# Turning the norms: tokens on partitions, fp16 rows turned by DMA transposes, in a fused conv/gMLP/MLP block

## The reference, cut to what matters

```
h  = rmsnorm(x, norm1_g);  p = h @ w_in                  # 1024 -> 2560
y_a = b_gate * conv3(c_gate * xc)                        # 512 channels
y_b = u * spatial_gating(layernorm(v))                   # 512 channels
y  = concat(rmsnorm(y_a), rmsnorm(y_b))
x1 = x + y @ w_out                                       # 1024 -> 1024
h2 = rmsnorm(x1, norm2_g);  a = relu(h2 @ w_up)          # 1024 -> 4096
out = rmsnorm(x1 + (a * a) @ w_down, final_g)            # 4096 -> 1024
```

## Time and profile before

| | us |
|---|---|
| device time, 3 runs | 1275.43, 1275.84, 1279.14 |
| median | 1275.84 |
| span of the profiled execution, core 0, first to last instruction | 1233.4 |
| spans of the eight cores | 1226.8 to 1233.4 |
| what the median has beside that span | 42.4 |
| TensorE busy in the span | 1195.1 (97%) |
| VectorE busy | 939.3 (76%) |
| ScalarE busy | 533.5 (43%) |

### The profile page before, as it was taken

The page is one execution under the profiler, slowest core; times in us unless marked ns, Lnnn a source line. Parts: engine busy times, 40 slices in busy tenths (PEclk is TensorE's granted clock), DMA queues, the critical chain, the costliest instruction groups (busy, mean ns, idle before and its releaser), DMA issues.

```text
span 1233.4 us, 19511 instructions; the slowest of 8 cores (1226.8 to 1233.4 us)
## 1 busy us (share of the span) xinstructions
PE 1195.1 (97%) x6264; PEld 584.4 (47%) x6264; DVE 939.3 (76%) x1460; ACT 533.5 (43%) x905; POOL 82.0 (7%) x144
## 2 busy tenths in 40 slices
PE   5899999999999999999999999999999999999994
PEld 3345645546556464444444444444444444444442
DVE  2799889898899997448879747868746877856745
ACT  4554664555644555045047116217305417504533
POOL 0101011010001100001100100000000000100000
PEclk8999999999999999999999999999999999999998
DMA  7977888696676869357898954667964655975424
GB/s 184 163 162 197 202 219 202 175 258 153 176 234 182 294 219 301 119 183 174 222 309 270 282 204 159 212 199 223 296 230 150 218 185 172 296 252 179 150 90 137
DMA packets 60084, 253.87 MB, mean 206 GB/s; under 512 B 6224, under 2 KB 8400, under 8 KB 59984
## 3 DMA queue, kind: packets, MB, share of 16 engines
q1 hardware_dynamic: 38800, 182.36, 43.7%
q0 software_dynamic: 21184, 70.26, 25.9%
HBM read 211.71 MB, written 65.01 MB: 224 GB/s over the span
## 4 chain that ended last, share of the span: by engine, by line
PE 88%; DMA 8%; DVE 1%; issue 1%; ACT 1%; SPq 0%; DVEq 0%; ACTq 0%; POOLq 0%
PE PS L506 88%; DMA XS_92<-x_s 2%; DMA oT<-RA 1%; DMA RA<-x_s 1%; DMA WCXB_51<-wcxb 1%; DMA WV<-wv 1%; DMA X_75<-xT 1%; DMA WCXB_53<-wcxb 1%; DMA WSB_107<-wst 1%; DMA X_76<-xT 0%; DVE RB L522 0%; DVE RA L522 0%; SPq L533 0%; DVE H_93 L525 0%; ACT DUMP_57 L513 0%
## 5 line engine op out<-in xcount | busy, mean ns | idle before, releaser
L522 DVE TENSOR_TENSOR RB<-PS,RB 128x512 f32<-128x512 f32 x128 | 88.2, 690 | 84.6 <-PE PS L506 82.3
L522 DVE TENSOR_TENSOR RA<-PS,RA 128x512 f32<-128x512 f32 x96 | 66.0, 689 | 58.4 <-PE PS L506 55.6
L506 PE MATMUL PS<-YN,WO 128*128 128x256 f16 x896 | 104.7, 273 | 1.0 <-DVE YN L522 0.8
L522 DVE TENSOR_TENSOR A_86<-A_86 128x512 bf16<-128x512 bf16 (+1 forms) x192 | 93.9, 506 | 12.8 <-ACT A_86 L513 8.3
L506 PEld LDWEIGHTS PS<-YN,WO 128*128 128x128 f16 x896 | 87.3, 98 | 20.6 <-issue 2.8
L513 ACT ACTIVATE SN_88<-PS 128x512 f32<-128x512 f32 x63 | 37.2, 594 | 109.2 <-PE PS L506 108.7
L506 PE MATMUL PS<-A_86,RING_80 128*128 128x512 bf16 x308 | 76.7, 379 | 2.4 <-DVE RB L522 2.4
L506 PE MATMUL PS<-A_86,RING_82 128*128 128x512 bf16 x308 | 77.2, 379 | 0.0
L506 PE MATMUL PS<-A_86,RING_83 128*128 128x512 bf16 x308 | 77.1, 379 | 0.0
L506 PE MATMUL PS<-A_86,RING_81 128*128 128x512 bf16 x308 | 76.3, 379 | 0.0
L506 PE MATMUL PS<-H_93,RING_80 128*128 128x512 f16 x308 | 75.4, 379 | 0.0
(11 more groups left out here) (237 smaller groups left out, 2078.4 us busy)
## 6 DMA issues: line engine op xcount, KB each, us to landing
RING_80<-ws_s SPq DMA_DIRECT2D x20, 896.0 KB, 5.9
RING_81<-ws_s SPq DMA_DIRECT2D x20, 896.0 KB, 6.3
RING_83<-ws_s SPq DMA_DIRECT2D x20, 896.0 KB, 6.5
RING_82<-ws_s SPq DMA_DIRECT2D x20, 896.0 KB, 5.6
RING_84<-ws_s SPq DMA_DIRECT2D x20, 896.0 KB, 6.2
RING_85<-ws_s SPq DMA_DIRECT2D x20, 896.0 KB, 6.2
ws_s<-PREP_70 SPq DMA_DIRECT2D x12, 896.0 KB, 5.7
ws_s<-PREP_69 SPq DMA_DIRECT2D x12, 896.0 KB, 6.0
```

The source lines that it names most:

```text
L506: ins = e.matmul(real(o_), lhsT=l, rhs=r, start=st, stop=sp, skip_group_check=True)
L522: dve(lambda e: e.tensor_tensor(out=out, in0=real(in0), in1=in1, op=op), reads, writes, n, rate, in0)
```

## The change

x, x1 and the result are now kept with **tokens on partitions**: chunk `s` of a tile is 128 tokens x 1024 channels, `rows(b, s)`.

- Norms: a token's sum of squares is the accumulator of one ScalarE Square over its row, rstd a [128x1] or [128x4] column. `stats` with `ONESD` stays for tile 0 alone, which is still loaded transposed (`xT0`), and the `ONESE` sums of y stay.
- x of tiles 1 to 7: `normed_rows` casts to fp16 with rstd as the scalar, into one of two buffers `HTK`; `turn` is a DMA transpose on the SP queue from there into `HT`, 4 a tile of 256 KB. For tile m+2 this is done during tile m. Tile 0's x is loaded a second time, by rows, for the residual.
- x1: `out_proj` has YN stationary (128 tokens) and WO moving (512 columns), so 56 matmuls of 512 columns stand for 112 of 256. It squares, casts and stores h2 as fp16 rows (`h2_d`) beside x1; `h2_part` is two DMA transposes of 512 KB and eight in-place gain multiplies. `XS`, `RSL` and `rs_d` are gone.
- Down: A2 stationary, weights moving. The loop is product by product over 4 token chunks with 4 sets of banks; one ring load (1 MB) is one product's weights, 7 a phase in place of 8 of 896 KB. In the last phase the last four products go chunk by chunk, and each chunk is finished at once.
- 28 of the weight combinations are made in the mixer and 4 in the first up phase; `schedule` has 40 tries in place of 120; an operation `group` lets the four transposes into one HT buffer not wait for each other.

```diff
@@ new helpers
+        def turn(out, in_, reads, writes, dkey, nbytes, group=None, margin=1.0):
+            S.add("sp", lambda e: e.dma_start_transpose(out=out, in_=in_), reads=reads, writes=writes, dma_key=dkey,
+                  nbytes=nbytes, occ=0.6, margin=margin, packet=1.0, group=group)
+        def squares(b, s, dump, acc, key):
+            act(dump[:, :, :], b[:, 2 * s:2 * s + 2, :], AF.Square, b.keys(2 * s, 2), dump.keys(0, 2) + [key],
+                n=2 * MT + 170, accum_out=acc)
+        def x_norm(m):
+            b, h = X[(m + 1) % 3], HT[m % 2]
+            for s in range(4):
+                i, ap, keys = normed_rows(b, s, SSX[:, s:s + 1], [("ssx", s)], True)
+                turn(h[:, :, 128 * s:128 * s + 128], ap, keys, h.keys(0, 8), ("xt", i), 2 * 128 * 1024, group=("ht", m))
@@ out_proj
-            for dc in (0, 2):
+            for u in range(2):
...
+                    pe(bank, [(bank[:, :], YN[:, b, k, 128 * u:128 * u + 128], WO[:, a, k, :], first and k == 0,
+                               last and k == 3) for k in range(4)],
...
-            rs = RS1[nxt("rs", 3)] if m + 1 < NMT else RS7
-            rstd(rs[:, :], stats(x, X1Q, 8, ONESD), MT, rs.keys())
-            dma("sp", rs_d[m], rs[:, :], rs.keys(), [("rsd", m)], ("rss", m % 2), 4 * 128 * MT)
+                rstd_rows(SS1[:, 2 * u:2 * u + 2], 2, keys, keys)
+                for h in range(2):
+                    s = 2 * h + u
+                    i, ap, hk = normed_rows(x, s, SS1[:, 2 * u + h:2 * u + h + 1], [("ss1", u, h)])
+                    dma("sp", h2_d[m, 128 * s:128 * s + 128, :], ap, hk, [("h2d", m, s)], ("hs", i), 2 * 128 * 1024)
@@ h2_part
+            for kk in range(2):
+                q = ((3, 2), (4, 1))[kk][h]
+                turn(H2[:, q, :, :], h2_d[m, :, 512 * kk:512 * kk + 512], [("h2d", m, s) for s in range(4)], h2k(q),
+                     ("h2t", q), 2 * 512 * 512, margin=4.0)
+                for k in range(4):
+                    scale(H2[:, q, k, :], pcol(G2, 4 * kk + k), h2k(q, k), MT)
@@ down, in place of down_unit and final
+        def down(finish):
+            chains = [{P1: bA, P6: bA, P7: bA, P4: bA, P2: bD, P5: bC, P3: bC}
+                      for bA, bC, bD in (banks_acd() for _ in range(4))]
+            adds = {P1: (0, 0), P2: (0, 0), P5: (1, 1), P6: (1, 0), P3: (1, 0), P7: (1, 1), P4: (0, 1)}
+            def step(p, w, s):
+                a, b = p
+                bank = chains[s][p]
+                pe(bank, [(bank[:, :], A2[:, q, b, 128 * s:128 * s + 128], w[:, q, :], p in (P1, P2, P5) and q == 0,
+                           p in (P2, P3, P4) and q == 7) for q in range(8)],
+                   [x for q in range(8) for x in a2k(q, b)] + w.keys(0, 8))
+                h, d_ = adds[p]
+                b, j = R[h], 2 * s + d_
+                tt(b[:, j, :], bank[:, :], b[:, j, :], ALU.add, bank.keys() + b.keys(j), b.keys(j))
+            together = 7 if finish is None else 3
+            for p in ORDER[:together]:
+                w = RD[use(1)[0]]
+                for s in range(4):
+                    step(p, w, s)
+                refill(1)
+            if finish is not None:
+                ws = [RD[i] for i in use(4)]
+                for s in range(4):
+                    for p, w in zip(ORDER[3:], ws):
+                        step(p, w, s)
+                    finish(s)
+        def gains(g, s):
+            for h in (1, 0):
+                squares(R[h], s, DUMPF, SSF[:, 2 * s + h:2 * s + h + 1], ("ssf", s, h))
+                rstd_rows(SSF[:, 2 * s + h:2 * s + h + 1], 1, [("ssf", s, h)], [("ssf", s, h)])
+        def piece(g, s, after):
+            for h in (1, 0):
+                b = R[h]
+                for d_ in range(2):
+                    j = 2 * s + d_
+                    stt(b[:, j, :], b[:, j, :], SSF[:, 2 * s + h:2 * s + h + 1], GFR[:, d_, :], ALU.mult, ALU.mult,
+                        b.keys(j) + GFR.keys(d_) + [("ssf", s, h)] + after, b.keys(j))
+                dma("sp", oN[2 * g + h, s], rows(b, s), b.keys(2 * s, 2), [("out", 2 * g + h, s)], ("os", h, s),
+                    4 * 128 * 2 * MT)
@@ start
+        load_x(0, gate)
@@ tile loop
+            if m + 2 < NMT:
+                x_stats(m + 2)
...
+            if m + 2 < NMT:
+                x_norm(m + 2)
             out_proj(m)
```

More of the change, by code:

```diff
@@ L127, in add @@
         for k in reads:
-            w = self.last_w.get(k)
-            if w is not None:
+            for w in self.last_w.get(k, ()):
                 deps[id(w)] = w
         for k in writes:
-            w = self.last_w.get(k)
-            if w is not None:
+            joins = group is not None and self.groups.get(k, (None, None))[0] == group
+            for w in self.groups[k][1] if joins else list(self.last_w.get(k, ())) + self.readers.get(k, []):
                 deps[id(w)] = w
-            for r in self.readers.get(k, ()):
-                deps[id(r)] = r
         for k in reads:
@@ L139, in add @@
         for k in writes:
-            self.last_w[k] = op
+            if group is not None and self.groups.get(k, (None, None))[0] == group:
+                self.last_w[k].append(op)
+                continue
+            self.groups[k] = (group, list(self.last_w.get(k, ())) + self.readers.get(k, []))
+            self.last_w[k] = [op]
             self.readers[k] = []
@@ L549, in warm, with stats @@
             pe(bank, [(bank[:, 0:128], ONESD[:, :], ONESD[:, :], True, True)] * n, ONES + reads)
-        def stats(src, q, n, ones, rows=2, first=False, behind=[]):
+        def stats(src, q, n, ones, rows=2, first=False):
             bank = bank8()
@@ L582, in load_x, with load_first, rows @@
                     chain.append(landed)
-        def stage0_stats(m, behind=[]):
-            return stats(X[(m + 1) % 3], XQ[m % 2], 8, ONESD, 8 if m < 2 else 2, m == 0, behind)
+        def load_first(js):
+            for j in js:
+                src = xT0[:, 2 * MT * j:2 * MT * (j + 1)].rearrange("p (k t) -> p k t", k=2)
+                dma("sp", X[1][:, 2 * j:2 * j + 2, :], src, [], X[1].keys(2 * j, 2), ("xf", j), 4 * 128 * 2 * MT,
+                    key=first())
+        def rows(b, s):
+            return b[:, 2 * s:2 * s + 2, :].rearrange("p a n -> p (a n)")
@@ new lines, in normed_rows @@
+        def normed_rows(b, s, col, reads, by_dve=False):
+            i = nxt("htk", 2)
+            if by_dve:
+                dve(lambda e: e.tensor_scalar(out=HTK[i][:, :, :], in0=b[:, 2 * s:2 * s + 2, :], scalar1=col,
+                                              scalar2=None, op0=ALU.mult),
+                    b.keys(2 * s, 2) + reads, HTK[i].keys(0, 2), n=2 * MT, rate=2)
+            else:
+                act(HTK[i][:, :, :], b[:, 2 * s:2 * s + 2, :], AF.Identity, b.keys(2 * s, 2) + reads,
+                    HTK[i].keys(0, 2), n=2 * MT, scale=col)
+            return i, HTK[i][:, :, :].rearrange("p a n -> p (a n)"), HTK[i].keys(0, 2)
@@ L594, in stage0_norm @@
             rstd(rs[:, :], bank, MT, rs.keys())
-            for k in range(0, 8, step):
-                normalize(HT[m % 2], X[(m + 1) % 3], rs, k, step)
+            for k in range(0, 8, 2):
+                normalize(HT[0], X[1], rs, k, 2)
         def halo():
@@ L674, in out_proj @@
             x = X[(m + 1) % 3]
-            half = MT // 2
-            for dc in (0, 2):
+            for u in range(2):
                 def prod(bank, p, first, last):
                     a, b = p
-                    pe(bank, [(bank[:, half * u:half * (u + 1)], WO[:, a, k, (dc + u) * 128:(dc + u + 1) * 128],
-                               YN[:, b, k, :], first and u == 0 and k == 0, last and k == 3)
-                              for u in range(2) for k in range(4)],
+                    pe(bank, [(bank[:, :], YN[:, b, k, 128 * u:128 * u + 128], WO[:, a, k, :], first and k == 0,
+                               last and k == 3) for k in range(4)],
@@ L834, in winograd @@
             add(0, d2, bA)
-        def down_unit(o_, s0, s1):
-            def prod(bank, p, first, last):
-                a, b = p
-                for hf, s in enumerate((s0, s1)):
-                    w = RING[s]
-                    pe(bank, [(bank[:, :], w[:, a, k, :], A2[:, 4 * hf + k, b, :], first and hf == 0 and k == 0,
-                               last and hf == 1 and k == 3) for k in range(4)],
-                       [x for k in range(4) for x in a2k(4 * hf + k, b)] + w.keys(a))
-            def addr(h, d_, bank):
-                tt(R[h][:, d_, :], bank[:, :], R[h][:, d_, :], ALU.add, bank.keys() + R[h].keys(d_),
-                   R[h].keys(d_))
-            winograd(prod, addr, o_)
@@ L1018, in build_program @@
                     prep_some(m)
-                if c == 1 and not last:
-                    b0 = stage0_stats(m + 1)
-            if not last:
-                stage0_norm(m + 1, b0, 2 if m == 0 else 4)
+            if m == 0:
+                x_norm(1)
             y_norm(YA, SQ[0], (3, 2))
```

(1 more changed line is left out.)

228 lines of the change are left out of this document (101 added, 127 removed).

## The result

On the chip of this comparison the changed kernel takes 1283.63 us in the median of 12 runs, the kernel before 1272.62 of 12: a ratio of 1.0089, 95% interval 1.005 to 1.0128, so slower by 0.9%.

A forecast was written before the change was run, and what follows sets the result against it. TensorE, busy for 97% of the span, was taken as the bound. 1233.4 - 9.3 - 0.9 - 1.8 + 6.6 - 7.2 = 1220.8 us, with 42.4 fixed 1263.2, so 1263; its own range 1255 to 1272, the stated range up to 1281.

The forecast's parts named there:

- ONESD, output projection, the gap at 626 us, -12.0: TensorE savings: 43 ONESD matmuls gone, -9.3 us; output projection in 512 columns, -0.9; gap at 626 us gone, -1.8.
- The tail, -7.2: After the last down matmul: the finish ends at 1226.2 instead of 1233.4 us, -7.2; at best -9, otherwise -4.
- The start, +6.6: Start: tile 1's x ready later, +3.5 us, and its transposes' DMA time at a copy's price, +3.1; between 0 and +15.9.
- the stated bound of four: Start: upper limit for the DMA price of tile 1's transposes, four times a copy, 12.4 us.
- two HTK buffers, two rounds: Start: tile 1's four transposes go through two buffers in two rounds of issue and landing; 16 matmuls after the gap, +3.5 us.
- A clock at the lower level after a longer gap at the start: Start: listed among the signs that would show the forecast wrong.
- The x transposes have a tile's time, some 50 us: Mixer: x's transposes have some 50 us before the convolution reads them, so they cost zero.
- Edges of h2: Group to group: four 512 KB transposes fit within 48.4 us of down matmuls, about 1.6 us plus some 5 landing each; hidden.
- The 42.4 us around the span, taken as fixed: Whole kernel: profiled span is 42.4 us under the median of 1275.84; this was added unchanged to the forecast span.
- R late: Rival, down phases: residual reload lands late, 5.6 us in three groups, +16.8, giving 1280; chance 0.16.
- slow transposes: Rival, edges between groups: 512 KB transposes too slow to hide, slower than before from 13.5 us each, 1377 at 21.6; chance 0.14.
- The start eats it: Rival, start: transposes at four times a copy and x's second load uncovered, 22.1 us for 6.6, giving 1278.7; chance 0.12.

The follow-up runs named there:

- e4: The changed kernel again with no edit, beside the kernel before on one chip: 1.0189 of the kernel before, best 1256.5 us against 1232.2.
- e3: The changed kernel with the planner told a higher price for transposes (3.5 times the bytes, longer queue hold, more margin): 1.0338 of the kernel before.
- e9: The changed kernel with the stores of h2's rows issued by POOL instead of SP: 1.0271 of the kernel before.
- e15: The changed kernel with four HTK cast buffers instead of two for tile 1: median 1333.5 us beside 1335.5 before, on a chip with a lower granted clock.
- e18: The changed kernel with no edit, on a chip with a lower granted clock: median 1341.5 us beside 1346.8 before.
- e11: The changed kernel with h2's stores by POOL and every x tile transposed by the host, rows loaded again: 1.0104 of the kernel before, best 1240.4 us.
- e1: The kernel before, run again with no edit and a fresh profile: 1235.1 us, ratio 0.9992; spans 1224.9 to 1233.6.
- e13: The kernel before with 50 idle products on DVE ahead of tile 1's norm and nothing of the change: 1.0313 of the kernel before, best 1263.4 us.
- e5: The changed kernel with only x's 28 transposes replaced by plain copies in 256 B pieces: 1.0378 of the kernel before.
- e6: The changed kernel with only h2's 16 transposes replaced by plain copies in 1 KB pieces: best 1254.0 us.

## Why the prediction was wrong

By its steps, with the trace of the changed kernel on the first chip and e4:

- *ONESD, output projection, the gap at 626 us, -12.0.* Right in kind. From 600 to 1200 us TensorE is without a gap in e4, with 2782 matmuls, 0.2157 us each, against 2768 before; 500 matmuls fewer on the page.
- *The tail, -7.2.* Right: 7.6 us from the last add in place of 15.4, so -7.8.
- *The start, +6.6.* Here the forecast fell. Its price for transposes was a copy's, "since only order and address differ". An estimate from the first chip's trace: the queue is busy for 0.588 x 1277.4 = 751 us; 198.1 MB of copies at 2.96 are 586; 165 us are left for 15.7 MB of transposes, 10.5 us per MB or 3.5 copies, in packets of some 250 bytes (62,700 more under 512 B, for 15.7 MB). The same sum gives 8.0 us per MB in e4 and 6.2 to 7.7 in e3, e9, e15 and e18, each time with all other bytes taken at a copy's 2.96. So it is 2 to 3.5 copies, and the stated bound of four holds. The larger error was to ask only when tile 1 would be ready. The text had "two HTK buffers, two rounds", and did not ask who is queued behind the third cast on DVE. It was tile 0's own work: 11 to 17 us idle at 60 to 100 us, at a clock of 0.78 to 0.87, where 1 to 2 were before. "A clock at the lower level after a longer gap at the start" was on the list of signs, but was given no price.
- *"The x transposes have a tile's time, some 50 us": zero.* 1.5 to 7.5 us of idle time at 140 to 380 us (0 to 2 before); e11 without them has 1.0 to 2.3.
- *Edges of h2.* Looked at between groups only, where e4 shows nothing. The first group's transposes run while the mixer still stores h2's rows on the same queue, and that edge was put at nothing without being looked at: 7 to 20 us idle at 440 to 500, most of it gone when the stores change queue (e9). Before, h2 was read by POOL (16 loads of XS); the change moved the reading onto SP, in front of the stores, and what else that queue carries at this moment was the question to ask.
- *The 42.4 us around the span, taken as fixed.* Wrong (e1): 1.6 us. The rest must have been another chip. It shifts the forecast for e4's chip to 1222 and says that the profile and the times were not one pair.

Over e4's eight cores the sum closes. In the mean a core has 33 us more of idle time than before (53 for 19 up to 1210 us). The mean span before is 1230.0; less 10.2 for the matmuls and 7.8 at the tail (the 1.8 at 626 us is idle time itself), plus 33, it is 1245. Measured is 1249.3, and the 4 us left go with the clock, 0.984 for 0.992. Of the 33 us the forecast had 6.6.

The rivals: *R late* did not come about, nor did *slow transposes*: 512 KB land in 6.9 us in the median, 23.8 at most, and from 600 to 1200 us TensorE waits neither for H nor for RA. *The start eats it* had one of the two right places and by luck near the right price (22.1 us), with a wrong reason: it added up the transposes' DMA time and the second load of x, and not what stands behind the third cast. Neither TensorE nor VectorE waits for a load of x by rows, and ScalarE for 1.2 us in all (core 5 of the changed kernel); what these bytes cost other transfers was not measured. None of the three had the mixer's end.

On the Trainium skill: "Advanced Engine Details and Errata", section "X-Bar Transpose (TRN2)", says such transposes are as fast as regular DMAs. Here they take 2 to 3.5 times a copy's engine time by the estimates above, and the measurement decides. "VectorE: DVE Perf Modes", section "The three transpose paths", gives 1309 ns a block; 16 blocks one after another would be 20.9 us, and 6.9 was measured for 512 KB in the median, so the blocks of one transfer do not go one after another at that price, though a single landing reached 23.8.

## What to carry over

Where a step gets a buffer ring through a DMA, write down for every wait on that ring who stands behind the waiting instruction on its engine and on the issuing queue; both losses here were of work that had nothing to do with the transposes. Look also at what else lies in a buffer's memory: at the mixer's end the waiting instruction was not the next cast but the first one of the next phase to use the same bytes. A gap in TensorE's work costs more than its length (30 us for 22 in e13): price the clock behind it. And check that a profile's span and the times it is set against belong together before calling their difference fixed.

## What was not expected of the hardware

- DMA transposes of 2-byte data go as packets of some 250 bytes and take an estimated 2 to 3.5 times the engines' time of a copy; 4.0 us per MB more than plain copies in small pieces (e4, e5, e6).
- The issuing queue is held by them. On SP (the HT and H tiles of the changed kernel; ns, least, median, most):

```profile
L598 SPq DMA_TRANSPOSE HT<-HTK x28: 1216/1318/4390, 64.1 to 380.8; - x28
L598 SPq DMA_TRANSPOSE H<-h_s x16: 1656/4160/11761, 392.9 to 1028.1; - x16
```

  The store of h2's rows has 338 in the median. 1.2 us is the least for 256 KB; with full DMA engines a 512 KB transpose holds the queue for 12 us, in e9 for 15.5. A plain load can do so too: one of 896 KB held it for 8.85 us at the same place.
- 22 us of idle time put into the kernel before, most of it at 22 to 100 us, cost it 30 us (e13), with its clock at 0.86 to 0.89 for 40 us on core 5.
- The kernel before takes 1233 to 1237 us on four chips at a mean clock of 0.99 and 1336 and 1347 on two at 0.90 to 0.96; where it takes 1272 its clock is not on record (the changed kernel's is 0.95 to 0.98 there, and 0.98 to 0.99 on e4's). A ratio of two kernels need not carry from one chip to another (1.0189 on e4's, 1.0089 on the first).
